# Layer norms of a two-block kernel: the sixth tile's offset added on VectorE, and the order of variance, mean subtraction and scaling

## What is computed

```
def layer_norm(x, g, b):
    mu = mean(x); var = mean(square(x - mu))
    return (x - mu) * rsqrt(var + eps) * g + b
h = layer_norm(ALPHA * h + 0.5 * swiglu(h, w_up, w_down), g, b)
h = layer_norm(ALPHA * h + mix, g, b)
```

## Time and profile before

| | us |
|---|---|
| median of 3 runs | 2468.93 (2468.43 to 2469.22) |
| the profiled execution | 2472.63 |
| its span | 2470.8 |
| PE busy | 2407.4 (97%) |
| DVE busy | 1720.5 (70%) |
| ACT busy | 1340.6 (54%) |
| granted TensorE clock, mean | 0.993 of full |

### The profile page before, as it was taken

The page is one execution under the profiler, slowest core; times in us unless marked ns, Lnnn a source line. Parts: engine busy times, 40 slices in busy tenths (PEclk is TensorE's granted clock), DMA queues, the critical chain, the costliest instruction groups (busy, mean ns, idle before and its releaser), DMA issues.

```text
span 2470.8 us, 48299 instructions
## 1 busy us (share of the span) xinstructions
PE 2407.4 (97%) x18906; PEld 2305.7 (93%) x18906; DVE 1720.5 (70%) x2565; ACT 1340.6 (54%) x2355; POOL 90.3 (4%) x101
## 2 busy tenths in 40 slices
PE   8999999999899999999999999999999999999998
PEld 8889999999899999999999997899999999789998
DVE  6788777776888867776766576576566656668665
ACT  5778655544588855564444445454444444555443
POOL 0000000000100000000010010010001001001000
PEclk9999999999999999999999999999999999999999
DMA  6454444455344444445455544345545554434553
GB/s 205 130 155 136 138 153 153 142 166 190 101 151 141 136 140 151 151 141 180 143 174 180 168 143 122 117 140 176 177 164 162 178 168 140 139 109 148 193 179 112
DMA packets 397976, 376.08 MB, mean 152 GB/s; under 512 B 27199, under 2 KB 396013, under 8 KB 397693
## 3 DMA queue, kind: packets, MB, share of 16 engines
q1 hardware_dynamic: 397821, 373.94, 47.9%
HBM read 372.84 MB, written 1.05 MB: 151 GB/s over the span
## 4 chain that ended last, share of the span: by engine, by line
PE 76%; DVE 14%; ACT 4%; DVEq 2%; DMA 2%; issue 1%; SPq 1%; ACTq 0%
PE ps L582 21%; PE ps L584 21%; PE ps L583 21%; DVE scratch L1793 3%; DVE w_lo L1570 3%; PE ps L803 1%; DVEq L1792 1%; PE ps L834 1%; PE ps L835 1%; PE ps L836 1%; ACT w_hi L1085 1%; ACT scratch L1085 1%; DVE xT L1695 1%; DMA raw<-in_ffn_w_up 1%; DVE xT L1692 1%
## 5 line engine op out<-in xcount | busy, mean ns | idle before, releaser
L1570 DVE TENSOR_TENSOR w_lo<-raw,w_hi 128x1024 fp32r<-128x1024 f32 x664 | 812.8, 1229 | 419.6 <-ACT w_hi L1085 418.1
L582 PE MATMUL ps<-x_hi,w_hi 128*128 128x256 f32 (+1 forms) x3664 | 1056.0, 288 | 13.5 <-DVE w_lo L1570 4.3
L583 PE MATMUL ps<-x_lo,w_hi 128*128 128x256 f32 (+1 forms) x3664 | 1043.6, 285 | 0.0
L584 PE MATMUL ps<-x_hi,w_lo 128*128 128x256 f32 (+1 forms) x3664 | 1040.4, 284 | 0.0
L1085 ACT ACTIVATE w_hi<-raw 128x1024 fp32r<-128x1024 f32 x664 | 697.4, 1055 | 442.5 <-PE ps L584 357.4
L582 PEld LDWEIGHTS ps<-x_hi,w_hi 128*128 128x128 f32 x3664 | 691.5, 189 | 39.4 <-issue 26.9
L583 PEld LDWEIGHTS ps<-x_lo,w_hi 128*128 128x128 f32 x3664 | 692.9, 189 | 2.1
L584 PEld LDWEIGHTS ps<-x_hi,w_lo 128*128 128x128 f32 x3664 | 694.6, 190 | 0.0
L582 PE MATMUL ps<-big_r,w_hi 128*128 128x272 f32 (+1 forms) x832 | 238.8, 287 | 0.0
L584 PE MATMUL ps<-big_r,w_lo 128*128 128x272 f32 (+1 forms) x832 | 238.1, 286 | 0.0
L1085 ACT ACTIVATE scratch<-ps 128x256 f32<-128x256 f32 (+9 forms) x328 | 122.8, 386 | 177.1 <-PE ps L836 77.5
(11 more groups left out here) (304 smaller groups left out, 3107.2 us busy)
## 6 DMA issues: line engine op xcount, KB each, us to landing
raw<-in_w_in SPq DMA_DIRECT2D x184, 512.0 KB, 4.8
raw<-in_ffn_w_up SPq DMA_DIRECT2D x176, 512.0 KB, 4.4
raw<-in_ffn_w_down SPq DMA_DIRECT2D x64, 512.0 KB, 4.2
raw<-in_mix_w_in SPq DMA_DIRECT2D x64, 512.0 KB, 4.6
scratch<-in_w_in SPq DMA_DIRECT2D x40, 512.0 KB, 4.8
raw<-in_w_mem_kv SPq DMA_DIRECT2D x32, 512.0 KB, 4.5
raw<-in_w_br_ssd SPq DMA_DIRECT2D x32, 512.0 KB, 4.1
raw<-in_ffn_w_down SPq DMA_DIRECT2D x32, 384.0 KB, 3.7
```

The lines of the kernel that those rows point to most:

```text
L582: mm(out, wh, xh, start=first, stop=False)
L583: mm(out, wh, xl, start=False, stop=False)
L584: return mm(out, wl, xh, start=False, stop=last)
L1570: tt(w_lo[:, p % PARTS, :, :], raw_at(slot_of(Q, p))[:, :, (p % 2) * P:(p % 2 + 1) * P], wh_f[:, p % PARTS, :, :], ALU.subtract).then_inc( ...
```

## The change

The offset of tile 6 is added to `off_sum` by DVE in a new function, and TensorE's product for it goes away. The sum's signal moves to the new function. TensorE takes the squares' first product ahead of the offset's first one, and the last tile's offset ahead of both last squares. In `layer_norm` the variance goes ahead of the first subtraction, and the three other subtractions are put between the scaled tiles; `lower` is issued in pairs, with `scaled` behind.

```diff
             def last_sums(T, NL, n):
-                off_part(T, 6, n)
+                off_part(T, 7, n)
                 square_part(NL, 6, n)
-                off_part(T, 7, n)
                 square_part(NL, 7, n)
                 keep_warm(WARM)
...
+                    square_first(NL, n)
                     off_first(NL, n)
-                    square_first(NL, n)
                     last_sums(T, NL, n)
...
-                tt(off_sum[:, 0:n], xT[:, 4, c], xT[:, 5, c], ALU.add).then_inc(S["off_summed"], 1)
+                tt(off_sum[:, 0:n], xT[:, 4, c], xT[:, 5, c], ALU.add)
...
+            def sum_sixth(NL, n):
+                c = slice(TOK2 - n, TOK2)
+                v.drain()
+                tt(off_sum[:, 0:n], off_sum[:, 0:n], xT[:, 6, c], ALU.add).then_inc(S["off_summed"], 1)
...
                 v.wait_ge(S["off_squared"], NL + 1)
-                less_offset(0)
                 v.wait_ge(S["var_done"], NL + 1)
                 tt(rstd[:, 0:n], ps[3][:, 0:n], off2[:, 0:n], ALU.subtract).then_inc(S["var_ready"], 1)
-                less_offset(2)
+                less_offset(0)
                 v.wait_ge(S["rstd_ready"], NL + 1)
                 v.reciprocal(rstd[:, 0:n], rstd_in[:, 0:n])
                 v.drain()
                 if final:
-                    for o in range(4):
-                        scaled(o)
+                    scaled(0)
+                    scaled(1)
+                    less_offset(2)
+                    v.drain()
+                    scaled(2)
+                    scaled(3)
                     less_offset(4)
                     less_offset(6)
                     v.drain()
...
                 scaled(0)
+                less_offset(2)
                 scaled(1)
+                lower(0)
+                lower(1)
+                scaled(2)
                 less_offset(4)
-                lower(0)
-                scaled(2)
-                lower(1)
                 scaled(3)
                 lower(2)
+                lower(3)
+                scaled(4)
                 less_offset(6)
-                scaled(4)
-                lower(3)
                 scaled(5)
                 lower(4)
+                lower(5)
                 scaled(6)
-                lower(5)
                 scaled(7)
                 lower(6)
                 lower(7)
...
                     if o == 6:
                         sum_squares(l, SEQ)
+                        sum_sixth(l, SEQ)
...
+                        if n == 3 and r == 4:
+                            sum_sixth(NL, size)
```

More of the change, by code:

```diff
@@ L981, in feed_forward @@
                             mean_tiles(NL, size)
+                square_first(NL, size)
                 off_first(NL, size)
-                square_first(NL, size)
                 last_sums(T + FT, NL, size)
@@ L2173, in _ @@
                         sum_squares(NL + 1, size)
+                        sum_sixth(NL + 1, size)
                     if o < KT - 1:
```

## The result

The changed kernel took 2477.33 us (median of 8 runs, 2474.71 to 2479.02) beside 2469.28 for the kernel before (8 runs, 2467.78 to 2472.8): ratio 1.0032, 95% interval 1.0022 to 1.0041, slower. In a later session it took 2475.79 beside 2469.29, ratio 1.0031 (1.0022 to 1.0041). The prediction was 2476.5, range 2470.5 to 2480.0, slower with a chance of 0.74. The profiled execution of the changed kernel took 2477.51 us, of which 2475.7 are span.

What follows compares the result with a forecast made beforehand. TensorE, busy 97%, was taken to bound the kernel, with idles behind the norms set by the end of VectorE's stream. Terms 1.27 + 3.58 + 1.81 + 1.20 - 0.28 = +7.6 on 2468.93 gave 2476.5 us, range 2470.5 to 2480.

Steps and rivals of the forecast that it cites:

- the forecasts of 1.81 and 0.40: Shift where the transfer chain ends in an idle, variance plus stream: norm 4 +1.81, norms 3, 5 and 6 +0.40 each.
- Part 1: VectorE's added sum for the sixth tile in projection norms 1, 2, 4, 7 delays the split by +0.51 us.
- Part 2: One product less, new order: variance +0.41 after the last sum in projection norms; TensorE's products -0.46 in feed-forward norms.
- Part 3: Variance ahead of the first subtraction: with add and products, variance starts +0.35 in projection norms, -1.06 in feed-forward norms.
- Part 4: VectorE's stream behind the reciprocal grows from 7.81 to 9.25, +1.44 (+1.46 at 272 columns); TensorE's first three tiles +0.92 (norms 1, 7).
- a term of 1.79: Shift forecast for norms 2 and 7, each: 0.35 for the variance plus 1.44 for the stream.
- Norm 1, predicted 1.27: Norm 1 goes by TensorE's end of the first tiles: 0.35 for the variance plus 0.92.
- A: Rival: behind the norms transfers have slack and TensorE's own feed decides; +3.5 us, 2472.4; chance 0.13.
- B: Rival: the first tile behind each norm decides; -2.1 us, 2466.9, or 2463.2 in a lower variant; chance 0.10.
- C: Rival: longer idles behind norms 2 to 7 bring TensorE's clock to half in more stretches; 2478.5 to 2480.5; chance 0.12.

Runs made afterwards that it cites:

- e3: Changed kernel with two subtractions under the square root, ahead of the reciprocal, and the old stream behind it; 2470.76 us, ratio 1.0005 to the kernel before.
- e4: Changed kernel with the fourth part's weight split issued ahead of the norm, in the seven norms that have one; 2474.08 us, ratio 1.0014 to the kernel before.
- e7: Changed kernel with the sixth square's product issued ahead of the seventh tile's offset product; 2472.56 us, ratio 1.0014 to the kernel before.
- e1: Kernel before with the change's new sums and product order alone, subtractions and stream as before; 2466.28 us, ratio 0.9986.
- e8: Kernel before with the change's new sums in every norm and the early weight split, old order of subtractions; 2473.28 us, ratio 1.0018.
- e12: Kernel before with only two products exchanged in every norm, the seventh tile's offset ahead of the sixth square; 2468.33 us, ratio 0.9998.
- e2: Kernel before with only the change's new order in VectorE's layer norm, products and sums as before; 2473.33 us, ratio 1.0017.
- e9: Kernel before with the new sums in the feed-forward norms alone, sixth square's product still ahead of the seventh offset's; 2467.68 us, ratio 0.9995.
- the control: The changed kernel run again unchanged in a later session; 2475.79 us, ratio 1.0031 to the kernel before.
- e5: Kernel before with the fourth part's weight split issued ahead of the norm; 2466.98 us, ratio 0.9988.

## Why the prediction was right, step by step

The mechanism was right where it can be checked cleanly: an idle at the end of the transfer chain behind `last_split`, moved by variance plus stream. In norms 4 and 5, where it took about the same time from `last_split` to ScalarE's start (6.57 and 6.61 before, 6.53 in both after), the forecasts of 1.81 and 0.40 met 1.77 to 1.92 and 0.38 to 0.50, and the rest of the period hardly changed (184.04 to 184.11 from the idle's end to the next norm's zero, in both kernels). That the total (6.5 and 8.0 in the medians, 7.6 forecast) came so near owes something to luck: norm 2 fell short of its term and norms 3 and 6 of theirs, norm 7 went beyond its own in the profiles, and norm 1 can't be read cleanly.

**Part 1, the add.** +0.51 predicted, +0.51 in the rows of norm 1, +0.51 to +0.53 behind the last projection matmul of norms 4 and 7. The drain ahead of the new add costs its 0.09 (615.25 + 0.43 to 615.77), and the split starts 0.08 before the add has ended. The Trainium skill ("VectorE: DVE Perf Modes", section "The DRAIN you can't avoid") says that the next operation waits until the pipe is empty, but that one which is not held back starts earlier; the trace agrees with the second half here. In norm 2 the add costs 0.87 in both profiles of the change, since VectorE stands 0.44 ahead of it with nothing that the profile shows to wait for ("issue"); e3, e4 and e7 have this gap, e1 and e8 don't. Why is open.

```profile
1219.58 0.43 DVE L1684 TENSOR_TENSOR scratch<-scratch 128x256 f32<-128x256 f32 x1
1220.45 0.43 DVE L1690 TENSOR_TENSOR scratch<-scratch,xT 128x256 f32<-128x256 f32 x1 [0.44 <-issue]
```

**Part 2, the products.** The 0.41 for the sixth square is right: e7 takes 0.45 back. What I missed is that the same exchange brings 0.46, since it lets the first subtraction of the order before run under the squares (e12).

**Part 3, variance first.** The sum came out near the mark (norm 4: +0.39, norm 7: +0.43 for +0.35; norms 3 and 5: -1.00 for -1.06; the step from product to variance is 0.11, not 0.04), but in a way that hid the overlap of its halves. Two norms were off: norm 2 with +0.78 for +0.35, by the gap of part 1, and norm 6 with -0.63 for -1.06, by a step of 0.48 from product to variance. The variance of norm 5 behind its last projection matmul: before 3.68, products exchanged (e12) 3.22, with the new sums (e1) 2.77, with the new DVE order alone (e2) 3.14, both 2.68. So once the products are exchanged, variance first is worth 0.09. This is why e1 and e2 don't add up: both gain the same half microsecond. In norms 4, 5 and 7 the overlap is 0.42 to 0.46, so in eight norms some 3.6 of the 5.0 to 6.6 that were missing; the rest is within the intervals.

**Part 4, the stream.** 9.25 predicted, 9.22 measured, with the four 0.18 waits at the places named. TensorE's pair step is 2.45 (625.76 to 628.21), forecast 2.46, but tile 2 starts 1.07 behind its `scaled`, not 1.17 (624.69 to 625.76), so tile 6 stands 7.27 behind tile 0 (623.40 to 630.67), where it stood 6.54 behind it: +0.73 for its start, forecast +0.84. The end of the first three tiles comes 0.84 to 0.86 later against their start in norms 1 and 7, forecast +0.92; 0.50 in norm 2, forecast 0.52; and 0.73 in norms 3 to 6, forecast 0.80. e3, which gives the old stream back and puts the third subtraction under the root, comes within 0.3 of its expected time and takes 4.8 to 6.4 of the loss away.

**Norms where the size was off.** Norm 7 shows 2.5 in the table for a term of 1.79: 1.86 at the first idle and 0.65 in a second one, 12.5 later. The rows are those of the changed kernel's TensorE behind norm 7.

```profile
2283.86 0.38 PE L582 MATMUL ps<-x_hi,w_hi 128*128 128x256 f32 x1 [1.19 <-DVE scratch L2020]
2296.34 0.38 PE L582 MATMUL ps<-x_hi,w_hi 128*128 128x256 f32 x1 [0.47 <-DVE scratch L2020]
```

The second can't be put down to the change: e9 and e12, whose norm 7 has the old stream and whose variance there is as before, show it too (0.45 and 0.37); the profiles of before, e1 and e7 don't. Against e9 norm 7 costs 1.87. Norm 2 was mis-sized: 1.79 predicted, 0.01 in the control against e9, 1.30 in the first profile. The time from SPq's record to ScalarE's start was 7.43 before (1235.80 to 1243.23), 6.53 in the changed kernel and 5.18 in the control; the later request got a quicker landing, which my sum held constant, and that more than made up for a variance 0.43 later than forecast (part 3). Norms 3 and 6, predicted +0.40, took 0.1 to 0.4 less than in before's profile for the same reason: the same two points lie 5.78 and 6.71 apart there, 5.23 and 5.64 in the changed kernel (and the idle behind norm 6, 1.27 in that profile, is absent in e9 and e1). Norm 1, predicted 1.27: in before's profile its last residual sum was 1.4 later behind the projection than in e9 (2.75, 1.33), in the first profile of the change 1.1 later than in the control (2.94, 1.84). ScalarE had waited longer for a landing some 9 us ahead of it in these two (4.50 and 4.34, against 3.69 and 3.72), so both are likely disturbed by a transfer. The control against e9 has +1.64 at the idle's end.

**The rivals.** A (the transfers have slack, TensorE's feed decides) fails for the changed kernel: norms 4 and 5 moved by 1.77 to 1.92 and 0.38 to 0.50, where A has 1.15 and -0.26, and in e2 they and norm 7 moved by 0.87 to 0.93, where A's prices give 0.3 to 0.4. (e1 can't tell, since stream and feed are old in it.) A's 2472.4 lies below all runs of the changed kernel. But once the split is early, A's price fits better, and the cost is still 7.1 (e4 beside e5). B (the first tile decides) would have had e2 no slower than before, and it is. C (the clock) is weighed with the control. Here are two stretches of 4 us behind TensorE's idle after norm 2, in the changed kernel and then in the control; columns as in the earlier trace rows.

```profile
1246.40:1250.40 4.00, 3.95 (x19) 3.95 (x20) 3.81 (x5) 1.73 (x4) 0.00 (x0) 0.57 0.13 36
```

```profile
1246.40:1250.40 4.00, 3.99 (x30) 3.81 (x31) 2.93 (x4) 1.49 (x3) 0.00 (x0) 1.00 0.49 163
```

The idle was 2.52 in the first and 1.15 in the second; the granted clock 0.57 (near the lower level, 1.2 GHz) and 1.00. The low stretch costs 1.3: from the idle's end to norm 3 it is 185.35 in the first and 184.04 in the second. But the kernel before had the same low stretch in its profile (185.36, behind an idle of 2.26), and behind norms 4, 5 and 7, where the idles did grow, the clock stayed at 1.00 in both profiles of the change. Only the low stretch ahead of the long idle behind norm 1 was longer in the first one (10.2, against 6.8 before and in the control); two windows of it:

```profile
638.00:642.00 4.00, 4.00 (x20) 4.00 (x20) 3.78 (x7) 2.73 (x6) 1.68 (x3) 0.50 0.00 0
642.00:646.00 4.00, 4.00 (x21) 4.00 (x20) 3.69 (x9) 0.41 (x2) 0.00 (x0) 0.50 0.73 230
```

In the kernel before and in the control the clock of 644 to 648 is back at 0.87 and 0.83. e9 has only 3.4 of it, so this length differs between profiles without the change, and C did not come true where I had put it. The Trainium skill ("TensorE: Matmul & The Clock Gate", section "HAM oscillation — how this bites in real kernels") has the clock fall to half over idles between bursts of matmuls. The rows agree at idles of 2.26, 2.52 and 2.89 (e12, clock 0.68 in the 4 us behind it), and behind one of 1.91 in e8; but behind 2.10 in e2, 2.21 in e9 and 2.23 in e8 the clock stayed at 1.00, so in these kernels the length of an idle alone doesn't tell.

## What to carry to other kernels

Work moved out of one wait must be priced in every stream that it is moved into: once the products were exchanged, the subtractions freed 0.09 ahead of the variance, and they cost 1.41 to 1.44 behind the reciprocal, where a weight slot was freed only at the stream's end. Taking that one wait away did not make the change cheaper, since the next wait followed TensorE's feed, and that was longer too. When an edit has two halves, run them apart and together, as gains that use the same cover don't add. Here the half that is worth keeping, one product less and the last mean product ahead of the squares, pays only in the norms behind a feed-forward part, where its add is hidden (ratio 0.9981 with it there alone; e1, with it everywhere, had +0.43 and +0.54 in norms 4 and 7).

## What the runs showed that I had not expected

- Behind norm 1 TensorE was busy 4.00 of each 4 us and its clock was 0.50 all the same, for 6.8 us in before's profile and 10.2 in the changed kernel's.
- The same transfer behind the same norm took 7.43, 6.53 and 5.18 from SPq's record to ScalarE's start, and an idle of TensorE is then 1 us longer or shorter; a single profile can't price such a chain to better than that.
- From the last square's product to the variance it is 0.11 in nearly all norms of the changed kernel, but 0.48 in norm 6, in both of its profiles, in e3 and in e7; in e2 such a step (0.46) stands in norm 2 instead. No row shows what it waits for; it stays open, as does the 0.44 ahead of norm 2's add.
- An order of the stream in which each `lower` stands one step later, which would avoid the 0.18 waits, was not tried.
